# Tile 0 of a fused transformer layer on one core: projection pieces between attention heads, key scores ahead of the next queries, first expert picks one head at a time

## The reference, cut to what matters

```python
proj = rms_norm(x) @ w_in                      # 2592 columns: q, k, v, gate, c_q, c_kv, k_pe
q_r, k_r = rope(q), rope(k)                    # retention, 8 heads of 64
s = einsum(q_r, k_r) * decay; ret_o = s @ v + (q_r * decay) @ state
y = group_norm(ret_o) * gn * silu(gate)
q_lat = (rms_norm(c_q) @ w_uq)[nope] @ w_uk    # latent attention, 8 heads
p = softmax((q_lat @ c_kv.T + q_pe @ k_pe.T) * scale); mla_o = (p @ c_kv) @ w_uv
h = x + concat([y, mla_o]) @ w_o
# expert lookup: 8 heads, 16 picks each, of 16384 experts
s = (rms_norm(h) @ w_q) . sub_keys             # 16 key-score blocks of 128
top_s, top_i = top_k(s, 16); cand = top_s[0][:, None] + top_s[1][None, :]
best = top_k(cand, 16); g = softmax(best)
a = gelu(x . u_tab[expert]) * g;  h += sum(a * v_tab[expert])
y = rms_norm(h) * lnf
```

## Time and profile before

| | |
|---|---|
| time, median of 3 runs | 1970.28 us (1970.02 to 1973.4) |
| profiled execution | 1971.54 us, its span 1969.8 us |
| busy, share of the span | PE 78%, DVE 63%, POOL 62%, ACT 13% |
| DMA engines | 391 GB/s mean over the span, 770.51 MB in all |
| busiest queue | q0, the gathers and GpSimd's loads: 688.61 MB, 88.2% |
| mean granted TensorE clock | 0.849 of full speed |

### The profile page before, as it was taken

One profiled execution on the slowest core, in us unless ns is written; L12 is line 12 of the kernel. 1 busy time (PEld: TensorE's weight loads), 2 busy tenths in 40 slices (PEclk: granted clock), 3 DMA queues, 4 the chain that ended last, 5 costly groups with the idle time before them and its releaser, 6 DMA issues.

```text
span 1969.8 us, 18897 instructions
## 1 busy us (share of the span) xinstructions
PE 1545.7 (78%) x6535; PEld 621.4 (32%) x6535; DVE 1242.1 (63%) x3197; ACT 263.2 (13%) x610; POOL 1228.0 (62%) x1306
## 2 busy tenths in 40 slices
PE   7897969976798868896988777778797676566677
PEld 4573435532343522232343521124354000000000
DVE  2469876599765685556655688975457954544420
ACT  2311112101121110020321001022111000000000
POOL 1124575666776655557666666775575777677773
PEclk9899889997799988997898976988898666766679
DMA  7849999999999999999999999999999999999997
GB/s 296 319 178 397 387 402 409 387 409 381 410 409 410 409 405 410 411 392 411 410 385 410 409 409 408 401 407 394 403 387 409 409 409 409 410 409 409 409 409 310
DMA packets 220448, 770.51 MB, mean 391 GB/s; under 512 B 26848, under 2 KB 33824, under 8 KB 219200
## 3 DMA queue, kind: packets, MB, share of 16 engines
q0 software_dynamic: 187136, 688.61, 88.2%
q1 hardware_dynamic: 31488, 78.04, 10.5%
q10 hardware_dynamic: 1728, 2.65, 0.4%
HBM read 762.01 MB, written 7.19 MB: 391 GB/s over the span
## 4 chain that ended last, share of the span: by engine, by line
PE 31%; DMA 29%; DVE 19%; POOL 13%; issue 6%; ACT 2%; SPq 0%; DVEq 0%; ACTq 0%; POOLq 0%
DMA rows<-in_v,pair_idx 24%; PE acc L1043 9%; POOL rows L685 7%; DVE rows L1733 7%; POOL rows L675 6%; PE F L727 4%; PE F L934 3%; DMA rows<-in_u,eidx 3%; PE F L972 3%; PE F L899 2%; PE acc L710 1%; PE F L854 1%; DVE work L1612 1%; DVE work L1620 1%; DVE work L1614 1%
## 5 line engine op out<-in xcount | busy, mean ns | idle before, releaser
L1733 DVE CUSTOM_DVE_ANT_0 rows<-rows,xps 128x1024 f32<-128x1024 f32 x640 | 763.6, 1218 | 419.8 <-DMA rows<-in_u,eidx 417.7
L1043 PE MATMUL acc<-rows,spread_w 128*32 128x512 f32 x2560 | 777.2, 739 | 316.8 <-DMA rows<-in_v,pair_idx 316.1
L675 POOL DMA_INDIRECT rows<-in_u,eidx x640 | 605.8, 947 | 335.6 <-issue 154.1
L685 POOL DMA_INDIRECT rows<-in_v,pair_idx x640 | 608.6, 951 | 300.4 <-issue 156.3
L1043 PEld LDWEIGHTS acc<-rows,spread_w 128*32 128x32 f32 x2560 | 111.6, 119 | 864.5 <-DMA rows<-in_v,pair_idx 711.0
L972 PE MATMUL F<-work,wblk 128*128 128x128 f32 x768 | 102.5, 293 | 16.0 <-DMA wblk<-in_w_q 14.0
L972 PEld LDWEIGHTS F<-work,wblk 128*128 128x128 f32 x768 | 96.1, 205 | 36.3 <-issue 19.9
L727 PE MATMUL F<-wblk,work 128*128 128x512 f32 (+1 forms) x192 | 80.4, 567 | 2.7 <-ACT work L1167 2.7
L934 PE MATMUL F<-w_o_all,work 128*128 128x512 f32 x160 | 76.9, 631 | 5.1 <-ACT work L1260 2.5
L727 PE MATMUL F<-wblk,hbuf 128*128 128x512 f32 (+1 forms) x96 | 48.0, 583 | 14.9 <-ACT work L1167 13.5
L1733 DVE DVE_READ_ACCUMULATOR2_ANT dots<- 128x1 f32 x640 | 52.4, 82 | 0.0
(11 more groups left out here) (279 smaller groups left out, 1420.8 us busy)
## 6 DMA issues: line engine op xcount, KB each, us to landing
wblk<-in_w_q SPq DMA_DIRECT2D x48, 512.0 KB, 7.6
wblk<-in_w_in SPq DMA_DIRECT2D x40, 512.0 KB, 6.8
rows<-in_u,eidx POOLq DMA_INDIRECT x640, 11.9
rows<-in_v,pair_idx POOLq DMA_INDIRECT x640, 12.2
rows<-in_w_in POOLq DMA_DIRECT2D x4, 2048.0 KB, 12.0
rows<-in_w_q POOLq DMA_DIRECT2D x12, 512.0 KB, 9.0
w_o_all<-in_w_o SPq DMA_DIRECT2D x8, 512.0 KB, 10.3
work<-proj_d SPq DMA_DIRECT2D x2, 1296.0 KB, 11.2
```

Source lines behind the costliest of these rows:

```text
L675: nc.gpsimd.indirect_dma_start(row_slot[u_place(n) % SLOTS], None, a["u"], bass.IndirectOffsetOnAxis(eidx[:, t % 2, pick:pick + 1], 0)).th ...
L685: nc.gpsimd.indirect_dma_start(row_slot[v_place(n) % SLOTS], None, a["v"], bass.IndirectOffsetOnAxis(pair_idx[:, t % 2, item:item + 1], 0) ...
L1043: last = mm(acc[lo:lo + ROPE, 512 * c:512 * c + 512], spread_w[:, g % 2, at:at + ROPE], row_slot[v_place(q) % SLOTS][:, 512 * c:512 * c + ...
L1733: v.tensor_tensor_reduce(row_slot[at % SLOTS], row_slot[at % SLOTS], xps[:, :], 1.0, 0.0, ALU.mult, ALU.add, dots[:, g % 2, k:k + 1]).then ...
```

## The change

- **Pieces.** The six projections are no longer whole. `first` takes a range of k. The q and k projections are cut in two halves with latent steps between them; the gate and value projections (now in this order) are cut into four column pairs each, and one pair stands behind each of the `attend` steps 0 to 7. Retention's steps move in between too: rotation in four parts on VectorE behind `attend` 0 to 3, `turn_qk` behind 4, `ret_scores` behind 5, `ret_sums` behind 8, `ret_norm` behind 9. Attention so starts before gate and values are projected.
- **`w_o` in another order.** The attention half (k 4 to 7) comes first and waits only for the copy `turn_mla`; then `turn_mix`, then the retention half.
- **Loads.** `w_uq`, `w_ukt` and `w_uv` are sent earlier; `w_o` and the kept query weights go out after the fourth projection instead of the sixth, ahead of `xs`. GpSimd waits for all attention values before it clears `spread_w`.
- **Key scores.** In every tile `key_scores` of a pair of steps stands ahead of the next queries instead of behind them.
- **First picks.** In tile 0 the chunks are one head, one head, two heads, four heads. Head 0 goes through its whole pick in `query` 3 and head 1 in `query` 4.
- **ScalarE.** The 16 scalings of the next two tiles' tokens (`scale_pair`) move from behind `w_o` to `query` 0.

```diff
-FIRST_ORDER = (4, 5, 0, 1, 2, 3)
+FIRST_ORDER = (4, 5, 0, 1, 3, 2)
+G_AT = 4
...
-        tail = tail[1:]
-        tail.insert(2, ("roots", 1, 0))
-        return ([("first", 0, 0), ("first", 1, 0), ("first", 2, 0), ("stats", 0, 0), ("latents", 0, 0), ("first", 3, 0),
-                 ("turn_c", 0, 0), ("first", 4, 0), ("rotate", 0, 0), ("q_rope", 0, 0), ("turn_qk", 0, 0), ("q_nope", 0, 0),
-                 ("ret_scores", 0, 0), ("first", 5, 0), ("ret_sums", 0, 0), ("q_lat", 0, 0), ("q_lat", 1, 0), ("expand", 0, 0), ("ret_norm", 0, 0),
-                 ("attend", 0, 0), ("attend", 1, 0)]
-                + [step for i in range(7) for step in (("attend", i + 2, 0), ("gate", i, 0))]
-                + [("gate_root", 0, 0), ("attend", HEADS + 1, 0), ("silu", 1, 0), ("roots", 0, 0),
-                   ("attend", HEADS + 2, 0)] + tail)
+        whole = lambda o: ("first", (o, 0, KD), 0)
+        first = lambda o, half: ("first", (o, 4 * half, 4 * half + 4), 0)
+        column_pairs = [("first", (o, k, k + 2), 0) for o in (4, 5) for k in range(0, KD, 2)]
+        beside = {0: [("rotation", 0, 0)], 1: [("rotation", 1, 0)], 2: [("rotation", 2, 0)], 3: [("rotation", 3, 0)],
+                  4: [("turn_qk", 0, 0), ("gate", 0, 0)], 5: [("gate", 1, 0), ("ret_scores", 0, 0)],
+                  6: [("gate", 2, 0)], 7: [("gate", 3, 0)], 8: [("ret_sums", 0, 0), ("gate", 4, 0)],
+                  9: [("gate", 5, 0), ("ret_norm", 0, 0)], 10: [("gate_root", 0, 0)]}
+        attention = []
+        for i in range(HEADS + 3):
+            attention.append(("attend", i, 0))
+            attention += column_pairs[i:i + 1]
+            attention += beside[i]
+        return ([whole(0), whole(1), ("stats", 0, 0), ("latents", 0, 0), first(2, 0), ("turn_c", 0, 0), first(2, 1),
+                 ("q_rope", 0, 0), ("q_nope", 0, 0), first(3, 0), ("q_lat", 0, 0), ("q_lat", 1, 0), ("expand", 0, 0),
+                 first(3, 1)] + attention
+                + [("turn_mla", 0, 0), ("w_o", 0, 6), ("silu", 1, 0), ("w_o", 1, 6), ("turn_mix", 0, 4), ("roots", 0, 0),
+                   ("w_o", 2, 6), ("w_o", 3, 6), ("roots", 1, 0)] + tail[6:])
...
-    return ((0, 2), (2, 2), (4, 4)) if t == 0 else ((0, 4), (4, 4))
+    return ((0, 1), (1, 1), (2, 2), (4, 4)) if t == 0 else ((0, 4), (4, 4))
...
+            sp.dma_start(w_uq[:, :, :], a["w_uq"].rearrange("(k p) n -> p k n", p=P)).then_inc(small_in[0], 16)
+            sp.dma_start(w_ukt[:, :, :], a["w_ukt"]).then_inc(small_in[1], 16)
+            sp.dma_start(w_uv[:, :, :], a["w_uv"].rearrange("(k p) n -> p k n", p=P)).then_inc(small_in[2], 16)
...
-            sp.wait_ge(mm_in, NIN)
...
+            sp.wait_ge(mm_in, 4)
             for k in range(KD):
                 sp.dma_start(w_o_all[:, k, :], a["w_o"][P * k:P * k + P, :]).then_inc(w_o_in, 16)
             for hp in range(Q_KEPT):
                 sp.dma_start(w_q_kept[:, hp, :], a["w_q"][hp]).then_inc(q_kept_in, 16)
+            sp.wait_ge(mm_in, NIN)
+            for t in range(1, TILES):
+                sp.dma_start(xs[t], a["x_all"][P * t:P * t + P, :]).then_inc(xs_in[1], 16)
...
+            pool.wait_ge(mm_pv, HEADS)
             nc.gpsimd.memset(spread_w[:, :, :], 0.0).then_inc(spread_zero, 1)
             for hp in range(HELD):
-                if hp == 6:
-                    pool.wait_ge(mm_pv, HEADS)
...
-            def project_first(o):
+            def project_first(o, k0, k1):
                 cb, buf = loads[o]
-                pe.wait_ge(win_in[buf], 16 * (1 + (o >= 4)))
-                if o >= 4:
-                    pe.wait_ge(ev_in, o - 3)
-                for k in range(KD):
+                if k0 == 0:
+                    pe.wait_ge(win_in[buf], 16 * (1 + (o >= 4)))
+                    if o >= 4:
+                        pe.wait_ge(ev_in, o - 3)
+                    if o == 5:
+                        pe.wait_ge(ev_v, 1)
+                for k in range(k0, k1):
                     if o == 0:
                         pe.wait_ge(xt_ok, k + 1)
                         if k == KD // 2:
                             pe.wait_ge(win_half, 16)
                     last = mm(banks[o % 4][:, 0:width[cb]], xt[:, k, :], win[buf][:, k, :],
-                              start=(k == 0), stop=(k == KD - 1))
-                last.then_inc(mm_in, 1)
+                              start=(k == 0), stop=(k == KD - 1), skip_group_check=True)
+                if k1 == KD:
+                    last.then_inc(mm_in, 1)
...
+                    if t == 0 and g >= 2:
+                        pe.wait_ge(ev_qk, g - 1)
...
+                if t == 0 and i in (0, 2):
+                    pe.wait_ge(ev_mix, 1 + i // 2)
+                elif i == 0:
+                    pe.wait_ge(ev_mix, 2 * (t + 1))
...
+                at = (2 * i + 4) % KD if t == 0 else 2 * i
+                for k in (at, at + 1):
...
+                        if i >= 2 and i % 2 == 0:
+                            key_scores(t, i // 2 - 1)
                         if i < HEADS:
                             query(t, i)
-                        if i >= 2 and i % 2 == 0:
-                            key_scores(t, i // 2 - 1)
...
-                if o == NIN - 1:
-                    act.wait_ge(ev_in, NIN)
+                if o == G_AT:
+                    act.wait_ge(ev_in, G_AT + 1)
...
+            def turn_mla():
+                act.wait_ge(mm_pv, HEADS)
+                copy(mix_t[:, 4:8, :], f4(3)).then_inc(ev_mix, 1)
...
+                        if t == 0 and i == 0:
+                            scale_pair(0)
...
-                        if t == 0 and i == 4:
-                            exp_gates(t, *chunks(t)[0])
+                        if t == 0 and i in (3, 5):
+                            exp_gates(t, *chunks(t)[i // 2 - 1])
...
+            def rotation(i):
+                s, d, m = (ap.rearrange("p (h c d) -> p h c d", h=2 * HEADS, c=2) for ap in (pj[:, 0:1024], qk[0], rtmp[0]))
+                cos, sin = mid(cos64[:, 0, :], 2 * HEADS), mid(sin64[:, 0, :], 2 * HEADS)
+                if i == 0:
+                    dve.wait_ge(consts_in[1], 16 * 4)
+                    dve.wait_ge(ev_in, 4)
+                    v.tensor_tensor(d[:, :, 0, :], s[:, :, 0, :], cos, ALU.mult)
+                    link(v.tensor_tensor(m[:, :, 0, :], s[:, :, 1, :], sin, ALU.mult))
+                elif i == 1:
+                    v.tensor_tensor(d[:, :, 1, :], s[:, :, 1, :], cos, ALU.mult)
+                    link(v.tensor_tensor(m[:, :, 1, :], s[:, :, 0, :], sin, ALU.mult))
+                elif i == 2:
+                    v.tensor_tensor(d[:, :, 0, :], d[:, :, 0, :], m[:, :, 0, :], ALU.subtract)
+                    v.tensor_tensor(d[:, :, 1, :], d[:, :, 1, :], m[:, :, 1, :], ALU.add).then_inc(qk_ok, 1)
+                else:
+                    dve.wait_ge(qk_ok, 1)
+                    v.tensor_tensor(three(kdec[0], HEADS), three(qk[0][:, 512:1024], HEADS), row(k_prompt[:, :], HD),
+                                    ALU.mult).then_inc(kd_ok, 1)
...
-                        if i == 3 or i == 5:
+                        if i in (3, 4) and t == 0:
+                            chunk = chunks(t)[i - 3]
+                            if i == 3:
+                                dve.wait_ge(ev_ps, 1)
+                            top16(range(2 * i - 6, 2 * i - 4), lambda i: sc[:, i, :], tv, ti)
+                            pairs(*chunk)
+                            top16(range(i - 3, i - 2), lambda i: candf[:, i, :], bv, bj)
+                            places(t, *chunk)
+                            for c in range(2):
+                                look_up(*chunk, c)
+                            gates(t, *chunk)
+                        elif i == 3 or i == 5:
```

More of the change, by code:

```diff
@@ L838, in expand @@
                 pe.wait_ge(small_in[2], 16)
-                pe.wait_ge(ev_s, 2)
                 for k in range(2):
-                    last = mm(banks[3], ckvt[:, k, 0:P], w_uv[:, k, :], start=(k == 0), stop=(k == 1))
+                    last = mm(banks[1], ckvt[:, k, 0:P], w_uv[:, k, :], start=(k == 0), stop=(k == 1))
                 last.then_inc(mm_v, 1)
@@ L1368, in _ @@
                         turn_mix(t)
-                    elif step == "w_o" and t == 0 and i == 1:
-                        scale_pair(t)
+                    elif step == "turn_mla":
+                        turn_mla()
                     elif step == "norm2":
```

64 lines of the change are left out of this document (27 added, 37 removed).

## The result

The changed kernel takes **1980.35 us** (median of 14 runs, 1975.48 to 1989.62), the kernel before, measured beside it, 1973.3. One of the 14 executions of the kernel before took 2683.65 us, and the ratio is of the fast ones alone. Forecast were 1973.1 and a range of 1964.5 to 1977.5. The profiled execution took 1978.9 with a span of 1977.1, against 1971.54 and 1969.8.

What follows compares the result with a forecast made beforehand. DMA bounds 400 to 1900 us, but VectorE's work before the gather at 241.77 us sets the end; +0.9 (`w_o`) - 2.9 (key scores) + 4.8 (picks) = +2.8 us, median 1973.1 us, range 1964.5 to 1977.5.

Steps and rivals of the forecast that it cites:

- term 2: Key scores ahead of queries: tile 0's come 2.9 us earlier; in tiles 1 to 4 nothing, give or take 1 us.
- Term 1: End of `w_o` on TensorE, before tile 0's key scores: 0.9 us later, with `w_o` starting at 84.7 us.
- Term 3: VectorE's first picks in tile 0: two one-head chunks take 4.8 us more than one two-head chunk, and nothing hides it.
- decisive gather: GpSimd's gather at 241.77 us, after a wait for a dot: its time sets the end, and it comes 2.8 us later.
- the first gather: Rival, chance 0.20: DMA bounds 150 to 229 us, so the first gather's 6.9 us earlier start is gained: 1963.4 us.
- `w_uq` landed: Load before `q_rope`: lands at 30.7 us, 1.0 us wait; rival, chance 0.18: lands at 33.0, total 1975.9 us.
- near 22: Alternative for the `w_uq` load: with equal queue shares it lands at about 22 us, without the wait: 1972.1 us.
- third rival: Lead-in pieces fit better, chance 0.12: no waits for loads, full clock through `w_o`, change of -0.1 us: 1970.2 us.

Runs made afterwards that it cites:

- e15: Kernel before, with key scores ahead of the queries in tile 1 alone: 1976.40 us, ratio 1.0019.
- e16: Changed kernel, with key scores behind the queries in tile 1 alone: 1976.59 us, ratio 1.0017 to the kernel before.
- e18: The changed kernel itself, run and profiled a second time: 1979.49 us, ratio 1.0041 to the kernel before.
- e10: e4 with ScalarE's copy of the attention output (`turn_mla`) ahead of its square root: 1964.48 us, ratio 0.9957 to the kernel before.
- e11: e10 with the small loads issued at the start, not after the first half weight block: 1965.25 us, ratio 0.9964 to the kernel before.
- e13: e10 with one-head instead of two-head first picks: 1972.09 us, ratio 0.9995 to the kernel before.
- e17: e11 with key scores behind the queries in tile 0 too: 1966.53 us, ratio 0.9967 to the kernel before.
- e4: Changed kernel, with two-head first picks and key scores ahead of the queries in tile 0 only: 1969.14 us, ratio 0.9976 to the kernel before.

## Why the prediction was wrong

The step that failed is the last but one of term 2: "In tiles 1 to 4 dots' and rows' units stand between, DMA is the bound: nothing, give or take 1 us." It costs 3.7 us (e15), 4.7 (e16 against e18), in tile 1: VectorE waits 5.3 to 6.1 us for the first gates' exponentials and the gathers behind it come 2.9 to 3.8 us later. I reasoned from the bound of the whole stretch of 400 to 1900 us. But from 425 to 505 us VectorE was busy 76.4 of 80 us, and DMA already dipped to 375 GB/s: in that part the DMA engines wait for VectorE, and what delays VectorE there delays the end. I had priced the new order by one wait for ScalarE's copy, 0.67 us, from tile 0, where weights are kept or lie in the row slots. In tile 1 that wait does not occur; the weights come through a ring, and what is put ahead of its reader delays the reload.

The other steps, one by one:

- *Term 1, +0.9:* right for this profile (+0.98), by two errors that cancel: `w_o` started at 83.20 and not 84.7, and the half clock cost 2.9 us (10.05 - 7.13) and not 1.9. As a statement on the kernels it rests on one execution of before that was 2.4 to 3.9 us quicker there than four others with the same lead-in.
- *Term 2 in tile 0, -2.9:* -2.5 at the first MAX8, in every profile; partly given back at the index transposes, which I had not priced.
- *Term 3, +4.8:* +5.1 in tile 0. At the end 6.1 to 9.1. That nothing hides it was right; whether it reaches the end at its own length stays open.
- *+2.8 at the decisive gather:* +3.5 in the profile, +0.4 in the second one of the same kernel (e18). The match is in part luck. "The time of that gather sets the end" is false as such: between it and the end lay 3.8 of the 7.3 us.
- *The rivals:* the first gather came 6.4 us earlier and brought nothing, GpSimd only waited longer for the dot. `w_uq` landed as forecast (at 30.13 for 30.7, wait of 0.92 us for 1.0; 28.4 to 30.7 in the eleven profiles with this order of loads), and not near 22. The clock of the third rival did not hold in the changed kernel; e10 shows what it is worth.
- *The basis:* of the 7.25 us between forecast and median, 3.0 are that the three times shown had a median of 1970.28, and the fuller set of the same kernel 1973.3. Without these 3.0 the time would lie at 1977.3, just inside the range. The difference itself, which is free of this, was forecast as 2.8 and is 7.9 (5.9 to 9.9); with the 3.7 us of tile 1 it would have been 6.5.

## What to carry to other kernels

Where an order is changed in a loop over tiles, each tile is a case of its own: look in its own window which engine has no slack, and follow the instruction that gets later through every in-order queue behind it. Work put ahead of the reader of a short ring delays the reload too, and no longer fills the wait for it. And when a term rests on the clock or on a load's landing, one profile is one draw: fixed sections repeat to 0.2 us, while what depends on these moves by 2 to 5.

## What the runs showed of the hardware

- The section bound by VectorE (101.6 or 106.7 to 106.9 us) and the one from `w_o` to the first MAX8 (12.3 or 14.8) repeat to 0.2 us across eighteen profiles, while `w_o`'s end moved from 100.5 to 105.5 among kernels with the same lead-in.
- After an idle 3.47 us TensorE's first 16 `w_o` products took 8.5 to 10.2 us, in nine profiles, and the next 16 7.13; after an idle 0.68 us both took 7.13 (e10, e11, e13, e17). The granted clock of 80 to 90 us was 0.66 to 0.88 in the one case and 1.00 in the other.
- The same 40 KB table, issued at 14 us, landed at 23.33 in the changed kernel and at 27.47 (e4) and 28.36 (e13) in the same order of loads, while large loads filled the engines (DMA share 0.99 to 1.02 from issue to landing).
- In a ring of three 512 KB blocks, 1.1 us of work moved from behind the reader to ahead of it lengthened the waits for weights in tile 1 from 5.5 to 8.8 us (changed kernel; e15 alike), and the granted clock of the ten us around them is lower (0.66 for 0.83, 0.83 for 1.00).
